# Expert weights loaded and released in halves, a pair's products ordered by tile size, and rotary halves exchanged by ScalarE copies

## The reference

```python
half = x.shape[-1] // 2
x1, x2 = xf[..., :half], xf[..., half:]
return jnp.concatenate([x1 * cos - x2 * sin, x2 * cos + x1 * sin], axis=-1)
```

```python
h = silu(einsum('nd,edf->nef', x, w_gate[g])) * einsum('nd,edf->nef', x, w_up[g])
y = y + einsum('nef,efd->nd', h * gate, w_down[g])
```

## Time and profile before

| | |
|---|---|
| median of 3 runs | 1285.54 us (1282.66 to 1286.66) |
| the profiled execution, its own time | 1284.15 us |
| its span, first to last instruction | 1282.8 us |
| PE busy | 1204.0 us, 94% of the span |
| DVE, ACT, POOL busy | 583.9, 397.9, 146.7 us |
| mean DMA rate over the span | 265 GB/s |
| experts of layer 0, from the first `up` to the last `down` | 427.28 to 665.77 us |
| experts of layer 1, end of the last `down` | 1270.75 us |
| units 5 to 11 of the projection | 712 to 767 us |

### The profile page before, as it was taken

The page is one execution under the profiler, slowest core; times in us unless marked ns, Lnnn a source line. Parts: engine busy times, 40 slices in busy tenths (PEclk is TensorE's granted clock), DMA queues, the critical chain, the costliest instruction groups (busy, mean ns, idle before and its releaser), DMA issues.

```text
span 1282.8 us, 20881 instructions
## 1 busy us (share of the span) xinstructions
PE 1204.0 (94%) x8548; PEld 738.2 (58%) x8548; DVE 583.9 (46%) x1163; ACT 397.9 (31%) x739; POOL 146.7 (11%) x184
## 2 busy tenths in 40 slices
PE   6999999999998899999999998989999799999996
PEld 5866679877776433333336776767777544333332
DVE  3764368774545522211236667546455541222122
ACT  3533323263443111111125334454444211111113
POOL 5220022111001011000002230001000101001000
PEclk9999999899999899999999999999999899999999
DMA  9575354368659389999974477703775748999994
GB/s 302 155 227 151 102 172 141 115 221 316 228 185 397 134 334 420 420 421 423 419 279 132 135 250 259 256 8 100 296 304 199 321 197 334 416 421 420 421 418 168
DMA packets 114028, 340.52 MB, mean 265 GB/s; under 512 B 7598, under 2 KB 75514, under 8 KB 86272
## 3 DMA queue, kind: packets, MB, share of 16 engines
q1 hardware_dynamic: 108752, 323.51, 67.1%
q0 software_dynamic: 4736, 14.42, 3.6%
q10 hardware_dynamic: 432, 1.11, 0.3%
HBM read 328.48 MB, written 10.54 MB: 264 GB/s over the span
## 4 chain that ended last, share of the span: by engine, by line
PE 76%; DMA 8%; DVE 7%; ACT 5%; issue 2%; POOL 1%; SPq 0%; ACTq 0%; DVEq 0%; POOLq 0%
PE ps L2369 15%; PE ps L614 9%; PE ps L615 8%; PE ps L616 8%; PE ps L2444 6%; DMA arena<-in_w_exp_up 6%; PE ps L2413 4%; PE ps L1530 3%; DVE wl L608 2%; PE ps L1544 2%; PE ps L1569 2%; PE ps L1615 2%; PE ps L1633 2%; DMA stg<-in_w_mem_o 1%; ACT wh L600 1%
## 5 line engine op out<-in xcount | busy, mean ns | idle before, releaser
L2369 PE MATMUL ps<-arena,mkv 128*64 128x512 f32 x1024 | 226.4, 594 | 9.0 <-DMA arena<-in_w_exp_up 8.5
L614 PE MATMUL ps<-bx,wh 128*128 128x320 f16 (+2 forms) x688 | 192.4, 287 | 10.7 <-DVE wl L608 4.1
L615 PE MATMUL ps<-bx,wh 128*128 128x320 f16 (+2 forms) x688 | 192.6, 287 | 0.0
L616 PE MATMUL ps<-bx,wl 128*128 128x320 f16 (+2 forms) x688 | 192.3, 287 | 0.0
L608 DVE SCALAR_TENSOR_TENSOR wl<-stg,wh 128x1024 f16<-128x1024 f32 x122 | 154.6, 1307 | 50.1 <-ACT wh L600 50.1
L600 ACT ACTIVATE wh<-stg 128x1024 f16<-128x1024 f32 x122 | 122.5, 1050 | 146.2 <-PE ps L616 127.8
L2369 PEld LDWEIGHTS ps<-arena,mkv 128*64 128x64 f32 x1024 | 75.6, 137 | 153.9 <-issue 152.2
L2584 DVE TENSOR_TENSOR arena<-ps,arena 128x512 f16<-128x512 f32 x64 | 44.1, 689 | 160.6 <-ACT arena L2530 113.5
L2588 DVE COPY arena<-ps 128x1 f32<-128x1 f32 x32 | 5.1, 159 | 185.3 <-PE ps L2391 185.3
L614 PEld LDWEIGHTS ps<-bx,wh 128*128 128x128 f16 x688 | 68.7, 101 | 34.9 <-issue 14.7
L614 PE MATMUL ps<-arena,wh 128*128 128x320 f16 x288 | 86.6, 301 | 0.9 <-ACT mkv L1212 0.9
(11 more groups left out here) (438 smaller groups left out, 1782.3 us busy)
## 6 DMA issues: line engine op xcount, KB each, us to landing
arena<-in_w_exp_gate SPq DMA_DIRECT2D x60, 1024.0 KB, 12.1
arena<-in_w_exp_up SPq DMA_DIRECT2D x60, 1024.0 KB, 14.2
arena<-in_w_exp_down SPq DMA_DIRECT2D x32, 1024.0 KB, 15.0
stg<-in_w_exp_down SPq DMA_DIRECT2D x32, 1024.0 KB, 16.3
arena<-in_cache_mem_k SPq DMA_DIRECT2D x16, 1024.0 KB, 8.0
arena<-in_cache_mem_v SPq DMA_DIRECT2D x16, 1024.0 KB, 5.0
stg<-in_w_in_a SPq DMA_DIRECT2D x28, 512.0 KB, 4.7
stg<-in_w_qkv_c SPq DMA_DIRECT2D x20, 512.0 KB, 3.6
```

Source lines behind the costliest of these rows:

```text
L614: nc.tensor.matmul(out, wh[:, s, at:at + 128], hi, start=start, stop=False, **flags)
L615: nc.tensor.matmul(out, wh[:, s, at:at + 128], lo, start=False, stop=False, **flags)
L616: return nc.tensor.matmul(out, wl[:, s, at:at + 128], hi, start=False, stop=stop, **flags)
L2369: last = nc.tensor.matmul(ps[64 * j:64 * j + 64, UB, :], xe[:, q % 2, j, k, :], gu[:, g % 2, j, :, k, :], start=(k == 0), stop=(k == KD - ...
```

## The change

Three things change; the merging of a few semaphores goes with them.

1. **Expert weights in halves.** Each pair's `gate` and `up` weights are loaded as two halves of the input channels, each of four DMAs of 512 KB, with a semaphore for each half (`gu_in`, `gu_hi`). `up` waits for the second half before its fifth step. The first half of a buffer is released after the fourth step of `up` (`gu_half`), the second as before (`gu_used`).
2. **A pair's products by tile size.** `combine` takes tile 2 first, then 0 and 1. `transpose_h(q)` comes ahead of both `down` halves, up to pair 12. ScalarE's `to_hidden` moves ahead likewise.
3. **Rotary halves.** For units 4 to 10 TensorE's product by `rot` goes. ScalarE copies the four groups of 32 partitions crosswise into `swapped(i)` (four copies of 32 x 640), after `split_hi` of the step. VectorE multiplies that by a sin whose sign is in the table, in one instruction of 640 elements. Unit 11 keeps the product, into PSUM banks 0 and 1.

```diff
-            if g >= 2:
-                sp.wait_ge(gu_used, g - 1)
-            parts = ((slice(0, 4), gu_in[g % 2]), (slice(4, 8), gu_tail)) if p == NPAIR - 1 else \
-                ((slice(0, 8), gu_in[g % 2]),)
-            for k, arrived in parts:
+            for k, arrived, used in ((slice(0, 4), gu_in[g % 2], gu_half), (slice(4, 8), gu_hi[g % 2], gu_used)):
+                if g >= 2:
+                    sp.wait_ge(used, g - 1)
                 for j in range(2):
                     for m, src in enumerate((w_gate_f, w_up_f)):
                         sp.dma_start(gu[:, g % 2, j, m, k], src[2 * g + j][:, k]).then_inc(arrived, 16)
...
-                if q % rounds == 0 and k == 4 and p == NPAIR - 1:
-                    pe.wait_ge(gu_tail, 64 * (l + 1))
+                if q % rounds == 0 and k == 4:
+                    pe.wait_ge(gu_hi[g % 2], 64 * (g // 2 + 1))
...
+                if k == 3 and q % rounds == rounds - 1:
+                    last.then_inc(gu_half, 1)
...
-            for i in range(3):
+            for i in (2, 0, 1):
...
+            transpose_h(q)
             down(q - 1, 0)
-            transpose_h(q)
             down(q - 1, 1)
...
+            to_hidden(q)
             y_high(q - 1, 0)
-            to_hidden(q)
             y_high(q - 1, 1)
...
-            if b == 0 and c["diff"] and len(set(first_banks(c))) == 4:
-                if f >= 2:
-                    pe.wait_ge(S["rot_done"], 14)
+            if b == 0 and c["diff"]:
+                pe.wait_ge(S["w_ev"], sum(UNIT["qkv"]))
...
-            if i >= 5:
-                rotate(i - 1)
-        rotate(11)
+        pe.wait_ge(S["w_ev"], QKV + 12)
+        for c in range(2):
+            nc.tensor.matmul(ps[:, c, 0:T], const("rot"), zc[:, qkv_chunk(11) + c, :], start=True, stop=True
+                             ).then_inc(S["rot_ps"], 1)
...
+            if 4 <= i < 11:
+                act.wait_ge(S["w_ev"], QKV + i + 1)
+                if i >= 6:
+                    act.wait_ge(S["rot_done"], 2 * (i - 5))
+                for g in range(4):
+                    to, of = slice(32 * g, 32 * g + 32), slice(32 * (g ^ 1), 32 * (g ^ 1) + 32)
+                    last = nc.scalar.copy(swapped(i)[to], zc[of, qkv_chunk(i):qkv_chunk(i) + 2, :])
+                last.then_inc(S["half_swap"], 1)
...
+                dve.wait_ge(S["half_swap"], i - 3)
+                link(V.tensor_tensor(turned, turned, const("sin").unsqueeze(1).to_broadcast([128, 2, T]),
+                                     ALU.mult))
```

More of the change, by code:

```diff
@@ L64, in constants @@
         if m % 64 < 32:
-            rot[m + 32, m] = -1
+            rot[m + 32, m] = 1
         else:
@@ L83, in constants @@
     put("cos", np.cos(ang).astype(f))
-    put("sin", np.sin(ang).astype(f))
+    put("sin", np.where(p[:, None] % 64 < 32, -np.sin(ang), np.sin(ang)).astype(f))
     put("before", (p[:, None] < p[None]).astype(f))
@@ L343, in build @@
     lt = sq[0:96, 5, :]
-    names = """const_in tab_in vec_in small_in x_in gate_in cst_ready vec_ps vec_ev tr_ps tr_ev w_hi w_lo w_used
+    SMALL = 16 * 5
+    names = """const_in vec_in small_in x_in gate_in cst_ready vec_ps vec_ev tr_ps tr_ev w_hi w_lo w_used
         w_ev in_hi in_lo sq_ready sum_ready std_ready xn_ready gate_ps gneg_ready gln_ready rows_ready
@@ L919, in mlstm_pool @@
         nc.gpsimd.memset(dmat[rows, :, 384:448], 0.0)
-        nc.gpsimd.memset(wlast[rows, :, 0:8], 0.0).then_inc(S["row_pad"], 1)
+        nc.gpsimd.memset(wlast[rows, :, 0:8], 0.0).then_inc(S["padded"], 1)
         pool.wait_ge(S["rows_ready"], 1)
@@ L941, in mlstm_pool @@
         pool.wait_ge(S["decay_ready"], 1)
-        nc.gpsimd.memset(vw[rows], 0.0).then_inc(S["row_pad"], 1)
-        pool.wait_ge(S["row_pad"], 2)
+        nc.gpsimd.memset(vw[rows], 0.0).then_inc(S["padded"], 1)
+        pool.wait_ge(S["padded"], 2)
         pool.wait_ge(S["ml_ev"], 1)
@@ L1887, in build, with swapped @@
     TURN_BANK = (7, 4)
-    ROT_BANK, ROT_LAST = (5, 6), (0, 1)
     rsin = xn[:, 0:2, :]
-    def rot_bank(i):
-        return ROT_LAST if i == 11 else ROT_BANK
+    def swapped(i):
+        return xn[:, 4 + 2 * (i % 2):6 + 2 * (i % 2), :]
     def skew(i, m):
@@ L1908, in qkv_pe @@
     def qkv_pe(pe):
[L1910 to L1917, removed]
         base = IN["qkv"][0]
@@ L1978, in cosines @@
             for c in range(2):
-                n, at = 2 * (i - 4) + c, qkv_chunk(i) + c
-                pool.wait_ge(S["rot_ps"], n + 1)
+                at = qkv_chunk(i) + c
+                if i == 11:
+                    pool.wait_ge(S["rot_ps"], c + 1)
+                else:
+                    pool.wait_ge(S["half_swap"], i - 3)
                 nc.gpsimd.tensor_tensor(zc[:, at, :], zc[:, at, :], const("cos"), ALU.mult).then_inc(S["rot_cos"], 1)
@@ L2007, in rope @@
         def rope(i):
[L2008 to L2012, removed]
+            turned = rsin if i == 11 else swapped(i)
+            if i == 11:
+                for c in range(2):
+                    dve.wait_ge(S["rot_ps"], c + 1)
+                    last = V.tensor_tensor(turned[:, c, :], ps[:, c, 0:T], const("sin"), ALU.mult)
+                link(last)
+            else:
+                dve.wait_ge(S["half_swap"], i - 3)
+                link(V.tensor_tensor(turned, turned, const("sin").unsqueeze(1).to_broadcast([128, 2, T]),
+                                     ALU.mult))
             if i == 10:
@@ L2020, in rope @@
                     dve.wait_ge(S["rot_cos"], n + 1 - (2 if i == 11 else 0))
-                V.tensor_tensor(zc[:, at, :], zc[:, at, :], xn[:, at_s + c, :], ALU.add).then_inc(S["rot_done"], 1)
+                V.tensor_tensor(zc[:, at, :], zc[:, at, :], turned[:, c, :], ALU.add).then_inc(S["rot_done"], 1)
         for i in range(12):
@@ L2622, in moe_pool @@
         M = ML[l]
-        pool.wait_ge(S["pk_ready"], 3 * l + (2 if rounds == 1 else 3))
+        pool.wait_ge(S["pk_ready"], 4 * l + (2 if rounds == 1 else 4))
         for q in range(1, NPAIR * rounds):
```

36 lines of the change are left out of this document (18 added, 18 removed).

## The result

The changed kernel takes 1289.33 us (median of 17 runs, 1286.51 to 1291.77) where the kernel before took 1285.31 (17 runs): a ratio of 1.0034, with a 95% interval of 1.0026 to 1.0042. It is 4.4 us slower by that ratio, where 12.1 us less were predicted (1273.4 us). The profiled execution spans 1286.0 us, against 1282.8.

What follows compares the result with a forecast made beforehand. TensorE was taken to bound most stages, with the DMA queue slightly slower in the experts. Rotary 6.9 us plus experts 5.2 us made 12.1 us, so 1273.4 us, within 1271.5 to 1275.5 (chance 0.5), outer range 1268.8 to 1278.5.

Steps and rivals of the forecast that it cites:

- Dearer transfers: Expert loads with 4 KB rows run at 414 GB/s instead of 421, losing 1.5 and 1.4 us in the layers.
- Earlier start: Expert weights asked for earlier close queue gaps; with faster pairs, 1.3 and 1.8 us gained in layers 0 and 1.
- Later need: At each layer's end TensorE needs the second half only 3.43 us into up; 2.5 us gained a layer.
- Products by tile size: In the experts, fewer tile-width changes save 0.2 us a pair, mostly hidden where the queue bounds.
- Rotary halves: In the projection, removing TensorE's rotary products for units 4 to 10 gains 6.9 us.
- ScalarE hides them: Four added copies a projection step, 2.5 us and at most 2.8, fit ScalarE's step with 1.3 us to spare.
- Transfers 3% dearer: Rival on expert loads: the gain is only 9.3 us, giving 1276.2 us; chance 0.13.
- Transfers no dearer: Rival on expert loads: 4 KB rows cost nothing, gain 15.9 us, giving 1269.6 us; chance 0.17.
- VectorE and ScalarE do not bound the middle steps of the projection: Denies two projection rivals: VectorE or GpSimd bounds, 1277 us, chance 0.12; ScalarE bounds, kernel slower, chance 0.03.
- The halves do nothing: Rival on the experts: the queue doesn't set a layer's end, about 2 us stay, 1277 us; chance 0.05.

Runs made afterwards that it cites:

- Run 5: Run 4 with expert gate and up weights loaded as eight 512 KB DMAs with 4 KB rows, still released and awaited as whole pairs; ratio 1.0046 to the kernel before.
- run 7: Run 4 with the loads of the first out_c unit moved ahead of the second block of cached keys; ratio 0.9969 to the kernel before.
- run 3: The kernel before with the rotary change alone and the merged semaphores; ratio 0.9994 to the kernel before.
- run 4: The changed kernel with the weight halves undone, product order and rotary copies kept; 1281.52 us, ratio 0.9974 to the kernel before.
- run 12: Run 5 with the two halves of each matrix asked for one right behind the other; ratio 1.0015 to the kernel before.
- run 10: The changed kernel without part 1, with 4 KB rows in 1 MB DMAs, each one matrix's half for both experts; ratio 1.0166 to the kernel before.

## Why the prediction was wrong, point by point

- **Dearer transfers: the step that failed.** The prediction took "414, 0.17 us more for 4 MB", 1.5 and 1.4 us in the two layers, with 3% as the bound. Run 5 measures 8.6 and 5.4 in its traced loops, and some 9 us for both layers by the times. The full queue is at the bound: 412 to 413 GB/s for a mix of 4 MB of short rows and 2 MB of long ones, 0.3 us a pair. But in layer 0 the larger part is outside of the full queue, first of all at its starts, and I had costed no start at all. My two windows with short rows were both taken in a full queue, which can't show it.
- **The wait that takes the place of the one removed.** "Earlier start" was costed as a gain alone, and I looked at the queue only. Pair 2's early release makes VectorE late, and TensorE waits 3.4 us for it and then runs at a lower clock: 5.5 us in layer 0. No rival had it.
- **Later need and earlier start.** Predicted were 3.8 and 4.3 us of gain together; 6.9 and 4.6 were measured against run 5, where the dear loads leave more to win. The stretch behind `up 12` was put at 60.8 us and is 61.2. The mechanism was right; of the 2.1 us gained there 1.4 are the halves' (62.6 us without them) and 0.7 the order's, where 2.25 and 0.25 were forecast.
- **Products by tile size.** 0.2 us a pair were predicted, 0.33 measured, with no new wait for VectorE ahead of the transposes of a steady pair. But they aren't where the prediction had them: `combine` falls from 2.40 to 2.28 us (forecast 2.15 to 2.3), the two `down` halves stay at 3.58 (forecast 3.4 to 3.5), and the transposes, which the sum didn't have, fall from 0.44 to 0.23. So that the total is near is partly luck. By itself the order gives 0.35%, 4.5 us, of which the loops show 1.1 + 1.5; where the rest comes from isn't shown, and the interval is 1.8 us to either side.
- **Rotary halves.** The sum of 6.9 us is right for the stretch that it is about, and run 7 shows it there to 0.1 us; the whole kernel doesn't gain it. What failed in the stretch is "ScalarE hides them": four copies take 2.93 us, over my 2.8, which its step does hide, but I didn't look at what the instruction in front of them waits for. With TensorE's shorter steps the first unit of `out_c` is due earlier, while its DMA still queues behind 3 MB of cached keys and values. That costs 2.0 to 2.4 us in the stretch in runs 3 and 4, the copies that then collide with GpSimd included. I had written that nothing but the next step's copies is queued behind the copies, and had not asked what they are queued behind.
- **The rivals.** *Transfers 3% dearer* had the right rate and a time 13 us too low. *Transfers no dearer* fell, and with it the rule that it names: the Trainium skill (DMA: Bandwidth & Descriptors, "Specifications") gives 512 B for the full rate, and rows of 4 KB run at 412 GB/s here where 8 KB run at 421. VectorE and ScalarE do not bound the middle steps of the projection; at its end ScalarE's wait does. *The halves do nothing* is wrong too: at the end of layer 0 they give 1.4 us.
- **What the sum left out.** The stretch between the first scores and layer 1's experts stood in no term, and takes 4.7 us more. The runs don't show why.

In all: the experts, parts 1 and 2, were to give 5.2 us, and part 3 6.9. Measured, part 1 costs 7.7 us, and parts 2 and 3 together give 3.3.

## What to carry to other kernels

Cost a split of a transfer from a trace that has the short rows where the queue starts as well as where it is full, and try the split first on those loads alone whose late half is on the path that sets the end (here the last four pairs; in the whole time their gain is within the intervals). A buffer released earlier makes a transfer start earlier: list everything else that needs the DMA engines in that stretch, the engines' own instructions included. And when TensorE's step gets shorter, go through each engine's order again for waits on DMAs that were just hidden before, since work added behind such a wait inherits it. Last, look at the stretches that you didn't touch: here the largest was 2 to 8 us longer in all changed kernels but one.

## What the runs showed of the hardware that I had not expected

- With the DMA engines 99% busy, the rate was 266 GB/s for 6 us after a dry queue when every other block of 4 KB was read in DMAs of 512 KB, and 421 with rows of 8 KB (452 to 458 us of runs 5 and 4). With both blocks asked for together it was 365 (453 to 459 us of run 12), and with every other block in DMAs of 1 MB 330 (run 10, engines 95% busy).
- VectorE stood idle for some 4.4 us with its input ready, when weights filled the queue. By the order in the trace it waited for its instructions, which no run takes alone.
- Loads into 64 partitions run at 213 GB/s.
- VectorE's `split_lo` takes 2.36 us for two halves where it took 3.24 in the plain step, and GpSimd's two cos products 1.68 where they took 2.67. The copies of ScalarE now come first, so that the two engines work one after the other: GpSimd's row for the same step is

```profile
733.65 1.68 POOL L1981 TENSOR_TENSOR arena<-arena,cst 128x320 f32<-128x320 f32 x2 [4.18 <-ACT bx L1954]
```

and VectorE's `split_lo` had ended at 732. The block that the prediction weighed was there before the change, and the change takes it away.
